# Recurrent attention of the second block in 8 units instead of 16

## What is computed

```
decay_d[t, s] = log-forget sums + input gate, for the keys s that direction d may see, else -inf
w_d = exp(decay_d - m_d),  m_d = row maximum of decay_d
p_d = w_d * (q k^T)                                 # the same q k^T in both directions
den_d = max(|sum_s p_d|, exp(-m_d + own decay))
h = (p_0 @ v) / den_0 + (p_1 @ v) / den_1
h = h * rsqrt(mean(h^2) + eps) * gain               # per head, then gated
```

## Time and profile before

| | |
|---|---|
| median of 3 runs | 2582.45 us (2582.16 to 2584.41) |
| span of the profiled execution (first to last instruction) | 2580.6 us |
| own device time of the profiled execution | not listed; the span is 1.85 us under the median of the runs |
| PE busy | 2479.3 us, 96% of the span |
| DVE busy | 1219.7 us, 47% |
| ACT busy | 866.1 us, 34% |
| mean granted PE clock | 0.993 of full speed |

### The profile page before, as it was taken

The page is one execution under the profiler, slowest core; times in us unless marked ns, Lnnn a source line. Parts: engine busy times, 40 slices in busy tenths (PEclk is TensorE's granted clock), DMA queues, the critical chain, the costliest instruction groups (busy, mean ns, idle before and its releaser), DMA issues. The chain is left out here.

```text
span 2580.6 us, 33146 instructions
## 1 busy us (share of the span) xinstructions
PE 2479.3 (96%) x12924; PEld 1653.7 (64%) x12925; DVE 1219.7 (47%) x2007; ACT 866.1 (34%) x1432; POOL 28.2 (1%) x57
## 2 busy tenths in 40 slices
PE   8999999999999999999899999999999999999997
PEld 6789998888888999888777887333333333333332
DVE  6557747765765764765544556222222212222123
ACT  6435555544445555534434444011000100001001
POOL 0000000000000000000000000000000000000000
PEclk9999999999999999999999998999999999999999
DMA  9664445774764443675431236999999999999975
GB/s 356 238 212 142 136 138 192 256 248 175 258 214 143 154 147 123 246 267 195 134 105 49 88 105 239 404 429 427 430 427 429 428 429 428 428 429 428 429 331 211
DMA packets 113470, 687.32 MB, mean 266 GB/s; under 512 B 20674, under 2 KB 22098, under 8 KB 87794
## 3 DMA queue, kind: packets, MB, share of 16 engines
q1 hardware_dynamic: 105840, 656.47, 65.5%
q0 software_dynamic: 7520, 29.37, 3.2%
q10 hardware_dynamic: 2, 0.01, 0.0%
HBM read 683.70 MB, written 2.11 MB: 266 GB/s over the span
## 5 line engine op out<-in xcount | busy, mean ns | idle before, releaser
L2602 PE MATMUL ps<-wexp_all_second,con_all_whole 128*64 128x512 f32 x3168 | 705.5, 595 | 28.6 <-DMA wexp_all_second<-in_w_lin 28.5
L2602 PEld LDWEIGHTS ps<-wexp_all_second,con_all_whole 128*64 128x64 f32 x3168 | 220.3, 137 | 469.4 <-issue 396.1
L299 PE MATMUL ps<-h_hi_first,w_hi_first 128*128 128x256 f32 x848 | 247.6, 292 | 1.0 <-DVE h_lo_first L254 1.0
L299 PE MATMUL ps<-hi_gu_first,h_hi_first 128*128 128x512 f32 x616 | 244.8, 397 | 1.5 <-DVE lo_gu_first L409 1.5
L301 PE MATMUL ps<-h_hi_first,w_lo_first 128*128 128x256 f32 x848 | 240.4, 283 | 0.0
L300 PE MATMUL ps<-h_lo_first,w_hi_first 128*128 128x256 f32 x848 | 240.4, 283 | 0.0
L301 PE MATMUL ps<-hi_gu_first,h_lo_first 128*128 128x512 f32 x616 | 240.2, 390 | 0.0
L300 PE MATMUL ps<-lo_gu_first,h_hi_first 128*128 128x512 f32 x616 | 240.1, 390 | 0.0
L409 DVE TENSOR_TENSOR lo_gu_first<-raw_gu_first,hi_gu_first 128x1024 fp32r<-128x1024 f32 x182 | 212.9, 1220 | 30.8 <-ACT hi_gu_first L404 30.8
L977 DVE TENSOR_TENSOR w_lo_first<-raw_first,w_hi_first 128x1024 fp32r<-128x1024 f32 x122 | 148.9, 1222 | 129.5 <-ACT w_hi_first L970 128.1
L404 ACT CAST hi_gu_first<-raw_gu_first 128x1024 fp32r<-128x1024 f32 x182 | 179.6, 1052 | 9.9 <-DMA raw_gu_first<-in_ffn_wgu 9.9
(11 more groups left out here) (488 smaller groups left out, 3920.5 us busy)
## 6 DMA issues: line engine op xcount, KB each, us to landing
wexp_all_second<-in_w_gate SPq DMA_DIRECT2D x64, 2048.0 KB, 23.0
wexp_all_second<-in_w_lin SPq DMA_DIRECT2D x64, 2048.0 KB, 25.6
wexp_all_second<-in_w_down SPq DMA_DIRECT2D x64, 2048.0 KB, 20.4
raw_gu_first<-in_ffn_wgu SPq DMA_DIRECT2D x154, 512.0 KB, 5.1
raw_first<-in_w_mix SPq DMA_DIRECT2D x138, 512.0 KB, 3.4
raw_d_first<-in_ffn_wd SPq DMA_DIRECT2D x60, 512.0 KB, 5.9
raw_second<-in_w_mix SPq DMA_DIRECT2D x57, 512.0 KB, 3.3
wada_first<-in_w_ada POOLq DMA_DIRECT2D x48, 512.0 KB, 5.7
```

Source lines behind the costliest of these rows:

```text
L299: nc.tensor.matmul(out, w_hi, x_hi, start=start, stop=False, skip_group_check=True)
L2602: mm = nc.tensor.matmul(dst[side(half), :], lhs(k), B.wexp[2 * "gld".index(kind) + part][:, k % 4, half * HALF:(half + 1) * HALF], start=( ...
```

## The change

The units become (head, query block): 8 of them. A unit computes the decays of both directions (into banks 2 and 3), the scores once, both maxima, both exponentials and both products with the scores. DVE then takes both reciprocals, scales the weights that span all 512 keys, and adds the other direction's scaled weights to them. The sum is transposed once and multiplied with the values once; `dve_add` becomes a plain copy. The keys are laid in the order tokens 0, context, tokens 1, so that either span is contiguous; the copy that stores the decays is done in two pieces for it. The slots are laid every 5 half-halves instead of 3 (2 or 3 halves between two slots, not 1 or 2). In a slot PE now does `pe_scores(j)`, `pe_turn(j-2)`, the half, and `pe_values(j-2)`, and ACT does `act_turned(j-2)` ahead of `act_exp(j)`.

```diff
-        self.units = [(h, qc, d) for h in range(ML_HEADS) for qc in range(TC) for d in range(2)]
+        self.units = [(h, qc) for h in range(ML_HEADS) for qc in range(TC)]
@@ pe_scores
+        for d in range(2):
+            row, (a, b) = d * ML_HEADS + h, self.span(u, d)
+            if u >= 1:
+                pe.wait_ge(self.s["l_exp"], 2 * u - 1 + d)
+            nc.tensor.matmul(self.decay(u, d), B.pick8[:, row:row + 1].broadcast_to([3 * E, P]), B.decay3[:, a:b],
+                             start=True, stop=False, skip_group_check=True)
+            nc.tensor.matmul(B.ps[:, 2 + d, diag:diag + P], B.ident16, B.mask16[:, d, :], start=False, stop=True, skip_group_check=True)
         if u >= 2:
             pe.wait_ge(self.s["l_gated"], u - 1)
+        nc.tensor.matmul(tiles(self.score(u))[:, 0:4:3, :], q_in, tiles(keys[:, 0:T]), start=True, stop=True, skip_group_check=True)
+        nc.tensor.matmul(self.score(u)[:, P:3 * P], q_in, keys[:, T:NT2], start=False, stop=True,
+                         skip_group_check=True).then_inc(self.s["l_scores"], 1)
@@ dve_max
+        for d in range(2):
+            self.nc.vector.tensor_reduce(self.stat(u, d), self.decay(u, d), AX, ALU.max, negate=True).then_inc(self.s["l_max"], 1)
@@ act_exp
+        if u >= 2:
+            act.wait_ge(self.s["l_turned"], u - 1)
+            act.wait_ge(self.s["l_gated"], u - 1)
+        for d in range(2):
+            act.wait_ge(self.s["l_max"], 2 * u + d + 1)
...
@@ dve_gate
+        for d in range(2):
...
+            dve.wait_ge(self.s["l_exp"], 2 * u + d + 1)
+            self.nc.vector.scalar_tensor_tensor(p, p, 1.0, self.score(u)[:, a:b], ALU.mult, ALU.mult,
+                                                accum_out=self.stat(u, 4 + d)).then_inc(self.s["l_weighed"], 1)
+        dve.wait_ge(self.s["l_weighed"], 2 * u + 2)
+        den = self.stat(u, 4, 2)
         ch.link(self.nc.vector.scalar_tensor_tensor(den, den, -1.0, den, ALU.mult, ALU.max))
-        ch.link(self.nc.vector.tensor_scalar(den, den, self.stat(u, 2), None, ALU.max))
-        self.nc.vector.reciprocal(self.stat(u, 3), den).then_inc(self.s["l_recip"], 1)
+        ch.link(self.nc.vector.tensor_tensor(den, den, self.stat(u, 2, 2), ALU.max))
+        ch.link(self.nc.vector.reciprocal(self.stat(u, 6, 2), den))
...
+        ch.link(self.nc.vector.tensor_scalar(whole, whole, self.stat(u, 6 + full), None, ALU.mult))
+        self.nc.vector.scalar_tensor_tensor(whole[:, a:b], other, self.stat(u, 6 + part), whole[:, a:b], ALU.mult,
+                                            ALU.add).then_inc(self.s["l_gated"], 1)
@@ dve_add
-        if d == 0:
-            self.nc.vector.tensor_scalar(out, self.B.ps[:, 7, 0:P], r, None, ALU.mult).then_inc(self.s["l_added"], 1)
-            return
-        dve.wait_ge(self.s["l_added"], u)
-        self.nc.vector.scalar_tensor_tensor(out, self.B.ps[:, 7, 0:P], r, out, ALU.mult, ALU.add).then_inc(self.s["l_added"], 1)
+        self.nc.vector.tensor_copy(out, self.B.ps[:, 7, 0:P]).then_inc(self.s["l_added"], 1)
@@ slots
-for _j in range(2 * TC * ML_HEADS + 3):
-    _h = 2 * ML_FIRST + (3 * _j) // 2
+for _j in range(TC * ML_HEADS + 3):
+    _h = 2 * ML_FIRST + (5 * _j) // 2
     ML_SLOTS[_h // 2, _h % 2] = _j
@@ mixer2_program, tensor
                     lstm.pe_scores(pe, j)
-
-            def ml_close(j):
                 if 2 <= j < n_ml + 2:
...
                     lstm.pe_turn(pe, j - 2)
-                if j >= 3:
-                    lstm.pe_values(pe, j - 3)
+
+            def ml_close(j):
+                if 2 <= j < n_ml + 2:
+                    lstm.pe_values(pe, j - 2)
@@ mixer2_program, scalar
+                    if ml is not None and 2 <= ml < n_ml + 2:
...
+                        lstm.act_turned(act, ml - 2)
                     if ml is not None and ml < n_ml:
...
-                    if ml is not None and 2 <= ml < n_ml + 2:
...
-                        lstm.act_turned(act, ml - 2)
@@ mixer2_program, vector, decay_parts
-                nc.vector.tensor_copy(B.decay_raw, ps[0:3 * E, 2, :]).then_inc(s["decay_out"], 1)
+                nc.vector.tensor_copy(tiles(B.decay_raw)[:, 0:4:3, :], tiles(ps[0:3 * E, 2, 0:T])).then_inc(s["decay_out"], 1)
+                nc.vector.tensor_copy(B.decay_raw[:, P:3 * P], ps[0:3 * E, 2, T:NT2]).then_inc(s["decay_out"], 1)
```

More of the change, by code:

```diff
@@ L1667 @@
 class Mlstm:
-    SEMS = "l_scores l_max l_exp l_gated l_recip l_turned l_probs_t l_out l_added "
+    SEMS = "l_scores l_max l_exp l_weighed l_gated l_turned l_probs_t l_out l_added "
     def __init__(self, nc, B, s):
         self.nc, self.B, self.s = nc, B, s
-        self.units = [(h, qc, d) for h in range(ML_HEADS) for qc in range(TC) for d in range(2)]
+        self.units = [(h, qc) for h in range(ML_HEADS) for qc in range(TC)]
         self.n = len(self.units)
[L1679 to L1686, removed]
@@ L1688, in width, with span, full @@
-    def width(self, u):
-        return sum(b - a for a, b in self.runs(u))
+    def span(self, u, d):
+        qc = self.units[u][1]
+        return {(0, 0): (0, 3 * P), (1, 1): (P, NT2)}.get((qc, d), (0, NT2))
+    def full(self, u):
+        return 1 - self.units[u][1]
     def score(self, u):
         return self.B.ps[:, 4 + u % 2, :]
[L1694 to L1701, removed]
@@ L1703, in pe_scores, with decay @@
-    def pe_scores(self, pe, u):
[L1704 to L1714, removed]
+    def decay(self, u, d):
+        a, b = self.span(u, d)
+        return self.B.ps[:, 2 + d, a:b]
@@ new lines, in prob, with stat @@
+    def prob(self, u, d):
+        a, b = self.span(u, d)
+        return self.B.prob[u % 2 if d == self.full(u) else 2 + u % 2][:, a:b]
+    def stat(self, u, j, n=1):
+        return self.B.l_stat[:, u % 4, j:j + n]
+    def pe_scores(self, pe, u):
+        nc, B, (h, qc) = self.nc, self.B, self.units[u]
+        lo, diag = (h % 2) * HD, qc * 3 * P
+        for d in range(2):
[5 more added lines that the diff above has]
+            nc.tensor.matmul(B.ps[:, 2 + d, diag:diag + P], B.ident16, B.mask16[:, d, :], start=False, stop=True, skip_group_check=True)
@@ L1715, in pe_scores @@
         if u >= 2:
             pe.wait_ge(self.s["l_gated"], u - 1)
[L1717 to L1722, removed]
+        q_in, keys = B.q10[lo:lo + HD, MLQ + h // 2, qc * P:(qc + 1) * P], B.kv[lo:lo + HD, MLK + h // 2, :]
@@ L1729, in act_exp @@
     def act_exp(self, act, u):
[L1730 to L1737, removed]
@@ L1739, in dve_gate @@
[L1739 to L1747 removed]
+        h, qc = self.units[u]
@@ new lines, in act_exp @@
+        if u >= 2:
[3 more added lines that the diff above has]
+            act.wait_ge(self.s["l_max"], 2 * u + d + 1)
+            j = qc * 2 * ML_HEADS + d * ML_HEADS + h
+            self.nc.scalar.activation(self.stat(u, 2 + d), self.stat(u, d), ACT.Exp, bias=self.B.own_decay[:, j:j + 1])
+            self.nc.scalar.activation(self.prob(u, d), self.decay(u, d), ACT.Exp, bias=self.stat(u, d)).then_inc(self.s["l_exp"], 1)
@@ new lines, in dve_gate @@
+    def dve_gate(self, dve, ch, u):
+        full, part = self.full(u), 1 - self.full(u)
+        for d in range(2):
+            a, b = self.span(u, d)
+            p = self.prob(u, d)
+            dve.wait_ge(self.s["l_exp"], 2 * u + d + 1)
[3 more added lines that the diff above has]
+        den = self.stat(u, 4, 2)
+        ch.link(self.nc.vector.scalar_tensor_tensor(den, den, -1.0, den, ALU.mult, ALU.max))
+        ch.link(self.nc.vector.tensor_tensor(den, den, self.stat(u, 2, 2), ALU.max))
+        ch.link(self.nc.vector.reciprocal(self.stat(u, 6, 2), den))
+        whole, other = self.prob(u, full), self.prob(u, part)
+        a, b = self.span(u, part)
+        ch.link(self.nc.vector.tensor_scalar(whole, whole, self.stat(u, 6 + full), None, ALU.mult))
+        self.nc.vector.scalar_tensor_tensor(whole[:, a:b], other, self.stat(u, 6 + part), whole[:, a:b], ALU.mult,
+                                            ALU.add).then_inc(self.s["l_gated"], 1)
@@ L1752, in pe_turn @@
             pe.wait_ge(self.s["l_probs_t"], u)
-        for j in range(self.width(u) // P):
+        for j in range(KT):
             at = slice(j * P, (j + 1) * P)
-            mm = self.nc.tensor.transpose(self.B.ps[:, 6, at], self.prob(u)[:, at], self.B.con("ident"))
+            mm = self.nc.tensor.transpose(self.B.ps[:, 6, at], self.prob(u, self.full(u))[:, at], self.B.con("ident"))
         mm.then_inc(self.s["l_turned"], 1)
@@ L1761, in act_turned @@
             act.wait_ge(self.s["l_out"], u - 1)
-        w = self.width(u)
-        self.nc.scalar.copy(self.B.prob_t[:, u % 2, 0:w], self.B.ps[:, 6, 0:w]).then_inc(self.s["l_probs_t"], 1)
+        self.nc.scalar.copy(self.B.prob_t[:, u % 2, :], self.B.ps[:, 6, :]).then_inc(self.s["l_probs_t"], 1)
     def pe_values(self, pe, u):
@@ L1769, in pe_values @@
             pe.wait_ge(self.s["l_added"], u)
-        tiles = [t for a, b in self.runs(u) for t in range(a // P, b // P)]
-        for j, t in enumerate(tiles):
```

(16 more changed lines are left out.)

20 lines of the change are left out of this document (10 added, 10 removed).

## The result

The changed kernel takes 2596.45 us (median of 5 runs, 2594.62 to 2599.31) against 2582.61 for the kernel before measured beside it (5 runs, 2582.16 to 2586.28): the ratio is 1.0048, 95% interval 1.0036 to 1.0059: slower, by half a per cent. That is 13.8 us by the medians; the forecast was 7.1. The median stands 0.45 us over the upper end of the range given (2596); the ratio put on the base of the prediction, 2582.45 us, gives 2594.8, just inside it. A second measurement, with other kernels beside it, gave 2596.94 against 2582.84, ratio 1.0055 (1.0041 to 1.0069).

A forecast was written before the change was run, and what follows sets the result against it. PE, busy throughout the stretch, was taken as the bound; -14.6 work, +18.6 waits, +0.1 copy and +3.0 clock falls summed to +7.1 us on 2582.45, giving 2589.5 us, range 2584 to 2596.

The forecast's parts named there:

- work taken from PE: On PE over the 8 units, fewer scores, transposes and value matmuls: together 14.6 us saved.
- waits in `pe_values`: PE waits for DVE's add of unit j-3 in the same slot; seven waits, together +18.6 us.
- decays' copy in two pieces: One more fixed cost on DVE ahead of the first scores: +0.1 us.
- falls of the clock: PE's clock drops to half at long waits; two falls at 1.5 us each taken: +3.0 us.
- The bound: In the mixer's unit stretch PE is always busy; a shift of the mixer's end shifts the kernel's end one for one.
- decays, masks, scores: On PE, two old units of 2.57 us become a new one of 1.74: 6.6 us saved over 8.
- turns: On PE, the three transposes of a 384-key unit go: 0.33 x 8 = 2.6 us saved.
- values: On PE, six matmuls over three key tiles go: 0.67 us x 8 = 5.4 us saved.
- The rival in which every long wait brings a fall: Clock falls at each of six long PE waits, 9 us: +13, 2595.5 us; chance 0.10.
- the forecast's own case: One to five falls of PE's clock at the waits, 2587.5 to 2594 us; chance 0.58.
- The untouched clock: Same PE waits but no fall of the clock: +4.1, 2586.5 us, within 0.2%; chance 0.27.
- The faster one: Wait in `pe_values` vanishes if DVE's chain behind the scores takes under 2.0 us, not 4.4: 2568 us; chance 0.05.

The follow-up runs named there:

- without waits: Changed kernel with PE multiplying values one slot later and slot 9 laid one half later: 2567.66 us, ratio 0.9945 to the kernel before.
- half-filled run: Changed kernel with two unread PE matmuls (one for the last unit) ahead of each wait in `pe_values`: 2590.54 us, ratio 1.0026 to the kernel before.
- the run without the scaling: Changed kernel without the last two `dve_gate` instructions, scaling and adding of the other direction: 2582.78 us, ratio 0.9997 to the kernel before.

## Why the prediction was right in kind and short in size

The stretches give the whole account, from the first decays to the merge, in profiled executions:

| term | predicted | measured | from |
|---|---|---|---|
| work taken from PE | -14.6 | -15.8 | 74.9 without waits, against 90.7 |
| waits in `pe_values` | +18.6 | +19.4 | 94.3 with waits half filled and full clock, against 74.9 |
| decays' copy in two pieces | +0.1 | +0.07, ahead of the stretch | 0.78 us on DVE from the copy's start to the next instruction, against 0.71 |
| falls of the clock | +3.0 | +8.0 | 102.3 against 94.3 |
| sum | +7.1 | +11.6 | 102.3 against 90.7 |

**The bound** was read rightly: PE was full and nothing else mattered, and the mixer's end carried through to the kernel's end (13.85 us at the first expert DMA, 12.2 us in the span; where the difference went is told under what stays open).

**The work taken away** was 1.2 us larger. These are the steps of each kind of matmul, added up over the stretch, before and in the version without waits:

| | before | without waits | difference | predicted |
|---|---|---|---|---|
| decays, masks, scores | 20.72 | 13.96 | -6.76 | -6.6 |
| turns | 6.13 | 3.25 | -2.88 | -2.6 |
| values | 11.71 | 6.46 | -5.25 | -5.4 |
| halves | 51.21 | 50.32 | -0.89 | nothing |

The halves are what the prediction's sum lacked. The first matmul of a half that follows other work has a step of 0.20 to 0.23 us, not 0.12; there were 27 such in the stretch before, and with fewer slots there are 19. Among the scores, the second direction's decays start 0.06 us behind the first's mask (1466.08 and 1466.14 above), where the scores start 0.15 us behind a mask in both kernels. A unit's scores take 1467.56 - 1465.90 = 1.66 us, not 1.74. What makes the one step shorter than the other was not tested.

**The waits** were the step that decided the sign, and it held. Predicted, in order: 2.4, 3.25, 3.25, 2.4, 2.4, 3.9, 1.0 us; in the trace 2.38, 3.29, 2.80, 2.38, 2.38, 3.95, 0.53. The two that are shorter have a fall of the clock between DVE's start and PE's coming. In slot 5 (from 1476.34 above) PE's scores ran into the fall and took 1478.51 - 1476.34 = 2.17 us instead of 1.66, while DVE's split and what follows it started from the end of the previous chunk as always. So 0.5 us of that fall's loss was hidden in the next wait. Without a fall there, the half-filled run has two equal waits (1.48 us) in these two slots, and the run without the scaling has 1.10 us as its seventh. The scaling took 0.49 us as its row had said, the add 0.62 as duration where 0.55 was taken, the copy 0.28, and PE started 0.15 us after the copy's end, where under 0.1 was taken from no row. The lower end of 0.35 us for the scaling stood on no row either; the measured 0.49 is far from it. That end was also counted over seven slots, though the seventh has no scaling. In the table the waits' term is 19.4, since fill and restarts after a wait are in it.

**The clock** is the term that was sized wrong: "I take two falls", +3.0. There were five, in both traces of the changed kernel, the last of them twice as long as the others, so six times the price of 1.5 us that the prediction had worked out; six times 1.5 is 9, and 8.0 was measured (1.5 us of the 20.5 at half clock lay inside waits, and some of the rest was hidden as just told). The price per fall held; the number did not. The rival in which every long wait brings a fall (+13, 2595.5 us) came nearest to the measured 2596.45, and I had given it a chance of 0.10; as a mechanism it is not quite what happened, since the first long wait brought no fall. Five falls were the upper edge of the forecast's own case, and five at 1.5 us would have made its sum +11.6, which is just what the stretch shows. That it agrees so well is in part luck: the work taken from PE was put 1.2 us too low, and that is set off by waits and falls that were also put too low, by 0.8 and 0.5 us. The reason for two, that the three longest waits were the likely ones, was not one that any row supported: waits of 2.38 us did it as well.

The Trainium skill, TensorE: Matmul & The Clock Gate, section "HAM oscillation — how this bites in real kernels", tells of a kernel whose bursts of matmuls are parted by DMA waits of about 3 to 5 us, and which starts each burst at the low clock. This trace agrees in kind, with a fall at five of its six long waits. Three of these five were shorter than in that example (2.80, 2.38 and 2.38 us), and one of 2.38 us brought no fall. The warning was worth more weight than it got, though the example itself speaks of longer waits than most of those that were foreseen here.

**The other rivals.** The untouched clock (+4.1, 2586.5 us) had its waits right and is what the half-filled run comes near in its profiled execution (2585.2). The faster one was refused for the right reason: the chain on DVE, from the end of the scores to the copy, was as long as its rows said. Its time, 2568, is near that of the version in which the wait is gone (2567.66, or 15.2 us under the kernel before beside it where 14.6 was the sum).

**What stays open.** In the profiled executions the 12.2 us can be followed: the stretch begins 2.2 us later (1439.1 against 1436.9), is 11.6 us longer, and what follows it is 1.65 us shorter. The clock fits both outer parts. Ahead of the stretch it stood at half for 13.7 us before and for 20.5 us after, behind it for 17.1 and 13.7 us (in both, the last 6 us at half clock are left out). By the loss of 1 - 0.12/0.21 per us that makes about +2.9 and -1.5 us, an estimate. In all kernels with the change the stretch begins later than before (1438.6 to 1443.3), with 17 to 27 us at half clock ahead of it. Whether these falls at other places are chance or come with the change was not tested; the instructions up to there are nearly the same, and the kernel before has only one trace. By the medians the changed kernel is 13.8 and 14.1 us over the kernel before, and those 2 us more have no trace. Nor is it known what makes one wait bring a fall and another not: 2.1 us did and 2.76 us did not in one execution.

## What to carry to other kernels

When a consumer is moved up by one step of a software pipeline, look at every semaphore it waits on for the place of the producer within *its* engine's step, not only for the step: a copy of 0.28 us at the end of a list behind work that depends on the same step cost 17.7 us here, and either end of it can be moved. DVE at 55 us of work in 102 us said nothing of this; an engine's mean load does not show an order that is wrong. And where PE is the bound, price a new wait at more than its length: here each us of waiting brought some 0.4 us more through the clock (8.0 for 19.4), and a trace of before in which PE never waits can't show that.

## What the runs showed that was not expected

- In the changed kernel's two traces the clock fell to half at five of the six waits of 2.4 to 3.95 us, between halves that keep PE full; without the scaling it fell at two waits of 2.1 us. In the profiled executions of the kernels whose longest wait was 1.84 us or less it fell at none.
- Work that nobody reads, put into a wait, is repaid: with 26 such instructions in the waits (12.5 us busy, about 11.2 us by their steps) the stretch was 8.0 us shorter in the traces, and the time 6.4 us by the medians. But it must be measured: matmuls of 512 float32 columns stepped 0.43 us an instruction, two instructions for each one written.
- The executions of all kernels spread by several us (the kernel before from 2578.46 to 2591.86 us beside these seven), more than the 0.2% taken as a bound before; the slowest two had a mean clock of 0.989, the fastest three 0.993 or 0.994. The stretches in the traces told kernels apart that the times could not.
